# One ScalarE copy for both heads' turned weights, in the two mixers' attention

## The reference, cut to what matters

```python
s = jnp.einsum('bhrnqc,bhrnkc->bhrnqk', qs, k3)
s = jnp.where(valid, s, NEG_BIG)
lse = jax.nn.logsumexp(s, axis=-1)
p = jnp.exp(s - lse[..., None])
o = jnp.einsum('bhrnqk,bhrnkc->bhrnqc', p, v3)
...
weights = jax.nn.softmax(jnp.stack(lses, axis=0), axis=0)
o = jnp.sum(weights[..., None] * jnp.stack(outs, axis=0), axis=0)
```

## Time and profile before

| what | before |
|---|---|
| time, median of 3 runs | 2382.29 us (2382.02 to 2385.28) |
| the profiled execution's own time | 2381.16 us |
| its span, first to last instruction | 2379.4 us |
| PE busy | 2231.5 us (94%) |
| DVE busy | 1316.7 us (55%) |
| ACT busy | 898.2 us (38%) |
| attention of layer 0, from the first scores to the last values | 263.2 to 323.0 us |
| attention of layer 1 | 956.7 to 1014.5 us |

### The profile page before, as it was taken

How to read it: one execution, slowest core, us unless ns; L and a number is a source line. 1 busy time by engine, 2 the same in 40 slices (tenths; PEclk the granted TensorE clock), 3 DMA queues, 4 the chain that set the end, 5 groups by cost and what they waited for, 6 DMA issues and landing times.

```text
span 2379.4 us, 33737 instructions
## 1 busy us (share of the span) xinstructions
PE 2231.5 (94%) x14488; PEld 1716.7 (72%) x14488; DVE 1316.7 (55%) x1927; ACT 898.2 (38%) x1327; POOL 214.4 (9%) x170
## 2 busy tenths in 40 slices
PE   6999899999999998899999998998899998999994
PEld 5778478888887876588888876465788657677672
DVE  6756555525536665746435455466533364677775
ACT  5422553212223323733222332244322224666663
POOL 1112000000010121010000010000000001122221
PEclk9999999999999999999999999999999999999997
DMA  4211112232322111022232221211211325689984
GB/s 159 71 54 36 54 53 90 89 106 89 106 89 89 54 43 47 36 73 105 90 105 89 106 75 56 97 63 54 73 55 38 117 88 197 251 337 356 343 331 177
DMA packets 51848, 270.21 MB, mean 114 GB/s; under 512 B 12144, under 2 KB 12272, under 8 KB 22512
## 3 DMA queue, kind: packets, MB, share of 16 engines
q1 hardware_dynamic: 41472, 256.67, 29.4%
q0 software_dynamic: 9216, 8.42, 1.0%
q10 hardware_dynamic: 1008, 2.92, 0.3%
HBM read 266.92 MB, written 26.21 MB: 123 GB/s over the span
## 4 chain that ended last, share of the span: by engine, by line
PE 83%; DVE 9%; ACT 5%; issue 2%; DMA 1%; POOL 0%; SPq 0%; DVEq 0%; POOLq 0%; ACTq 0%
PE psum L123 80%; PE psum L126 3%; DVE A_mix L136 2%; DVE A_second L136 1%; ACT A_mix L130 1%; DVE A_mix L156 1%; ACT WH L130 1%; DVE WL L136 1%; DVE A_second L144 1%; ACT A_mix L133 1%; DMA raw<-in_w_in 0%; DVE A_mix L162 0%; DVE A_mix L153 0%; ACT A_second L130 0%; DVE A_second L150 0%
## 5 line engine op out<-in xcount | busy, mean ns | idle before, releaser
L136 DVE TENSOR_TENSOR WL<-raw,WH 128x1024 fp32r<-128x1024 f32 x236 | 298.7, 1268 | 397.5 <-ACT WH L130 397.1
L130 ACT ACTIVATE WH<-raw 128x1024 fp32r<-128x1024 f32 x236 | 248.2, 1054 | 415.6 <-PE psum L123 394.3
L123 PE MATMUL psum<-HH,WH 128*128 128x512 f32 x736 | 305.6, 415 | 32.4 <-DVE HL L144 18.7
L123 PE MATMUL psum<-R_op,WH 128*128 128x512 f32 x1024 | 315.9, 390 | 0.0
L123 PE MATMUL psum<-R_ffn,WH 128*128 128x512 f32 x1024 | 315.1, 389 | 0.0
L123 PE MATMUL psum<-HL,WH 128*128 128x512 f32 x736 | 292.7, 398 | 0.0
L123 PE MATMUL psum<-HH,WL 128*128 128x512 f32 x736 | 292.1, 397 | 0.0
L123 PEld LDWEIGHTS psum<-R_op,WH 128*128 128x128 f32 x1024 | 192.2, 188 | 40.7 <-issue 1.0
L123 PEld LDWEIGHTS psum<-R_ffn,WH 128*128 128x128 f32 x1024 | 192.2, 188 | 40.0
L123 PEld LDWEIGHTS psum<-HH,WH 128*128 128x128 f32 x736 | 141.8, 193 | 80.1 <-issue 31.8
L123 PE MATMUL psum<-A_mix 64*128 64x64 f32 (+5 forms) x1984 | 165.9, 309 | 35.5 <-DVE A_mix L136 22.2
(11 more groups left out here) (199 smaller groups left out, 2933.4 us busy)
## 6 DMA issues: line engine op xcount, KB each, us to landing
ring_moe<-in_w_gu SPq DMA_DIRECT2D x64, 1024.0 KB, 9.9
raw<-in_w_in SPq DMA_DIRECT2D x42, 1024.0 KB, 4.8
raw<-in_w_up SPq DMA_DIRECT2D x32, 1024.0 KB, 4.8
raw<-in_w_down SPq DMA_DIRECT2D x32, 1024.0 KB, 4.8
ring_moe<-in_w_dn SPq DMA_DIRECT2D x32, 1024.0 KB, 5.0
raw<-in_w_out SPq DMA_DIRECT2D x12, 1024.0 KB, 4.9
kept<-A_second SPq DMA_DIRECT2D x20, 256.0 KB, 2.1
raw<-in_dft SPq DMA_DIRECT2D x4, 1024.0 KB, 4.7
```

What stands on the lines that cost most here:

```text
L123: return self.raw.matmul(o, l, r, start=start, stop=stop)
L130: return self.raw.activation(o, i, f, scale=scale)
L136: return self.raw.tensor_tensor(o, a, b, op)
```

## The change

The four `PT` tiles are laid out as two pairs, at the same addresses as before. In the mixers' attention ACT issues one copy per step, 128 x 1024, from banks 2 and 3 to the pair, in place of two of 128 x 512. It waits for the transposes of head 1 (and so for those of head 0). The semaphore is counted up once per step; `mark` gives head 0's name to the same count. The wait for the values of step p-4, which stood behind that for head 0's transposes, stands ahead of it. The latent attention has no pair and keeps its two copies.

```diff
-            m.PT = [ar.take(S) for _ in range(4)]
+            m.pair = [t3(ar.take(2 * S), 2) for _ in range(2)]
+            m.PT = [m.pair[i // 2][:, i % 2, :] for i in range(4)]
...
+        s2.pair = None
...
-                    for hh in range(2):
-                        e.wait_ge(*at("att_pe", ly, "t", p - 2, hh))
-                        if p >= 4:
-                            e.wait_ge(*at("att_pe", ly, "o", p - 4))
-                        e.act(m.PT[p % 2 * 2 + hh][:, 0:kl], bk(B[2 + hh])[:, 0:kl], ACT.Copy).then_inc(
-                            *did("att_act", ly, "pt", p - 2, hh))
+                    if p >= 4:
+                        e.wait_ge(*at("att_pe", ly, "o", p - 4))
+                    if m.pair:
+                        e.wait_ge(*at("att_pe", ly, "t", p - 2, 1))
+                        e.act(m.pair[p % 2], psum[:, B[2]:B[2] + 2, :], ACT.Copy).then_inc(*did("att_act", ly, "pt", p - 2, 1))
+                        mark("att_act", ly, "pt", p - 2, 0)
+                    else:
+                        for hh in range(2):
+                            e.wait_ge(*at("att_pe", ly, "t", p - 2, hh))
+                            e.act(m.PT[p % 2 * 2 + hh][:, 0:kl], bk(B[2 + hh])[:, 0:kl], ACT.Copy).then_inc(
+                                *did("att_act", ly, "pt", p - 2, hh))
```

## The result

The changed kernel is slower: 2388.78 us, median of 22 runs (2385.56 to 2392.49), against 2382.33 us for the kernel before, also 22 runs. The ratio is 1.0029, 95% interval 1.0023 to 1.0035, so +5.5 to +8.3 us. The forecast was 2386.2 us, within 0.2% of before, in a range of 2383.0 to 2390.0. The time lies in the range; the case that I held likeliest, "not to be told from no change", is not the one that came.

The account below looks back on a forecast made before the run. PE was taken to bound the kernel, with ACT's copy holding it only at places in the two attentions. Layer 0's 1.76 and layer 1's 2.19 us sum to +3.95, predicting 2386.2 us, range 2383.0 to 2390.0.

Parts of the forecast that it names:

- not to be told from no change: Whole kernel: time within about 0.2%, 4.8 us, of before; chance 0.66, of which the forecast itself (+3.0 to +4.8) 0.52.
- the release: PE's transposes in the two attentions start 1.06 us after the copy's start, not 0.63: 0.43 us later for head 0.
- The six bare waits behind takings out: PE's starts hanging directly on a pair's first copy, three places per layer: 0.43 us more idle at each.
- The seventh: PE's bare wait for the copy at layer 1's opening (965.25 to 965.88): 0.43 us later there, 0.69 for the opening.
- The dear copy: Rival: crossing from bank 2 to 3 costs a start, release 1.21 us after the start; +6.9, 2389.2 us; chance 0.12.
- cycle: Four steps between takings out: 0.43 less 0.06, so 0.37 us more each; two per layer, 0.74 a layer.
- opening: From Fourier's last HH to the first taking out: 0.26 us more in layer 0, 0.69 in layer 1.
- end: From the third taking out on: net 0.37 for its stall, then 0.17 and 0.22 in the last copies; 0.76 us a layer.
- The clock: Rival: longer PE idle at the third taking out brings low clock, 2.0 us a stretch; 2388.2 or 2390.2 us; chance 0.17.
- The sign of failure that I had named: In the timeline: forecast falls if low-clock stretches come or go elsewhere by more than 2 us.
- The small gain: Rival: the larger operation pays, ACT free sooner, 0.06 us at six takings out; 2381.9 to about 2382.3 us; chance 0.08.

Follow-up runs that it names:

- fill_changed: The changed kernel with 10 identity transposes at three places of each attention where PE idles 1.4 to 2 us; ratio 1.0022, +5.2 us against the kernel before.
- fill_before: The kernel before with the same 10 identity transposes at the same three places of each attention; ratio 1.0001, +0.2 us against the kernel before.
- late_step14_only: The kernel before, but PE's turning of head 0 in step 14 also waits for head 1's copy; ratio 1.0015, +3.6 us against the kernel before.

## Why the prediction came out as it did

**What bounds, and the release: right.** The single copy was put at 1.01 us and took 1.00; the release at 1.06 us after its start, and it was 1.06. The six bare waits behind takings out grew by 0.43 as worked out (0.29 to 0.72 us, and 1.55 to 1.98). The seventh, in layer 1's opening, was hidden by a low stretch in this profile; where the opening was filled (fill_changed) it is 0.72 too. The dear copy, my first rival, is out: crossing the banks costs nothing.

**The stages: right in sum.** At full clock the working gives 2.19 us for a layer with a bare opening; fill_changed less fill_before gives 2.10 in both. By stage, in the distances of the table: cycle +0.31 (0.37 expected; the stalled transposes run in 1.09 and not 1.14 us, since head 1 is ready as soon as head 0), opening +0.54 (0.69 less the 0.06 by which HH comes sooner, 0.63), end +0.94 (0.82 expected). So 4.2 us for two layers with full clock, against 4.38 by the working. The forecast's 3.95 comes from giving layer 0's opening only 0.26, as its low clock covers a part of the loss. That is so, and by more than I had: where the low stretch fell in both kernels, the openings differ by 0.1 us or less (means of 23.75 in four of changed, 23.70 in two of before), not by 0.54.

**The clock: here a step failed.** I had it as a rival of 0.17 which comes or doesn't, with 2.0 us a stretch, and argued against it that PE had idled 1.55 us there and kept its clock. With 1.55 us or less of it, or filled, none of 16 ends had the low clock (only four of them are at 1.55 unfilled); with 2.0 us, 8 of 12 had it, for 1.2 to 1.6 us each. At that rate it is 2 layers x 8/12 x 1.4, some 1.9 us on average; by the changed kernel's own four ends, two of which had it, 1.3. What I called a rival belongs in the sum with its rate. The forecast lay 0.8 us under the bound of 0.2%, so that a term of 1.3 to 1.9 us decided on which side of it the time fell.

**Adding up.** Two profiles of each kernel allow a direct sum. From Fourier's last HH to the last taking out, both layers together, before took 117.6 us twice, the changed kernel 124.0 and 124.4: +6.6 us, where the medians of 22 runs differ by 6.45. Of these, 1.3 are the four cycles, 1.9 the two ends at full clock, 1.3 the low clock in the ends, and 2.1 the openings. The first three follow from the late release. The openings' part does not follow in full: it comes from four low openings of four against two of four. Were these as frequent in both kernels, the sum would be 4.5 us (always) to 5.5 (never), or 5.1 to 6.1 with the ends' clock at 1.9; the measured interval is 5.5 to 8.3. That the change makes low openings more frequent isn't shown; it can't do so by its waits in the same opening, as the stretch falls ahead of the first copy.

**The rest of the profiled difference.** The spans differ by 5.4 us: layer 0's attention +2.89 (62.69 against 59.80), layer 1's +3.54 (61.33 against 57.79; its opening has a low stretch that before's had not), and outside them -0.68 ahead of the first, -3.13 between and +2.81 behind, where the instructions are the same in both. These follow where low stretches fell: between the attentions there were 17.1 us of low clock in place of 23.9, behind them 76.7 in place of 70.4. The sign of failure that I had named, stretches coming or going elsewhere by more than 2 us, was there twice; that the two nearly cancel is luck. Over the fourteen profiles, the stretch between the attentions takes 627.6 us with 10.2 us of low clock, 630.6 to 630.9 with 17.1, 632.1 with 20.5 and 633.7 with 23.9. All that lies outside the attentions takes 2255.9 to 2267.7 us, in no order of the kernels. So a single profile can't show a difference of 2 us in its span, and that is why the stage table was needed.

**The small gain** did not come: ACT is free 0.06 us sooner (HH 0.90 us behind the copy's start in place of 0.96), which is worth 0.06 a cycle at most. With the second pair of banks it stays as 0.06 (13.02 against 13.08).

**Two rules beside the rows.** PE was idle 0.43 us longer at 290.77, while ACT is busy for 38% of the span. The Trainium skill (Perfetto Trace Analysis, "Optimizing Scalar/DVE Operations") says that where an unsaturated engine causes bubbles, broken-up instructions may let work complete sooner; the trace agrees. Eight of twelve ends were at the lower clock behind 2.0 us of idle time. The Trainium skill (TensorE: Matmul & The Clock Gate, "Part 1: The HAM clock gate") says that the clock drops after idle time; the runs agree that it can, and that 1.55 us did not do it in the four ends of before.

**What stays open.** Whether fill_before gains the 2 us of its openings: +0.2 was measured, and the interval allows it. Whether low openings come oftener in the changed kernel. Low stretches outside the attentions varied most between profiles, and no run here controls them.

## What to carry to other kernels

Two copies of 0.5 us each are not one of 1.0 if another engine waits for the first: ask who is released by which half, and count the half's duration at each place where the wait is bare. Freeing a second pair of banks took the copy off PE's path, and then one copy was as good as two. And where PE already waits long between short bursts of work, a little more waiting can cost a multiple through its clock: 0.48 us more cost 2.0 in late_step14_only, 1.5 of them by the clock. Work without a result, put in the wait, kept the clock in all six ends and six openings where it stood.

## What the hardware showed that I had not expected

Lengthening one wait of PE from 1.55 to 2.03 us, once a layer, made the end of the attention 2.0 us longer in both layers of the profile, 1.5 of them by the clock (granted clock 0.74 in the 4 us around it, 1.00 before). Ten transposes of the identity, 1.31 us, in the like wait of the changed kernel kept both its ends at full clock. In the openings, where PE waits about 1.5 us twice with 1.1 us of work between, the clock fell in 18 of 22 unfilled attentions, and in none of 6 filled ones; against the filled opening of the same kind it cost 1.0 to 2.5 us each. Between the attentions, 13.7 us more of low clock came with 6.1 us more of time. An ACT copy of 1024 columns across two banks takes 1.00 us, and 1.03 behind an idle time, where the line through the 256- and 512-column copies of the earlier trace rows gives 1.03.
